# One transformer block on one Trainium2 core: the first tile's projections and front alone at the start, the other tiles' projections moved behind them

## What is computed

```python
n = rms_norm(h, g_mix)
proj = n @ w_in                                   # 2832 columns
gq, gk, gv, gz, gb, ga, sq, sk, sv = split(proj)  # gq, gk, gv: 3 x 512; the other 1296 are "token" columns
qkv = silu(causal_depthwise_conv(concat(gq, gk, gv), conv_w))      # 4 taps over tokens
o_gdn = gated_delta_net(qkv, gz, gb, ga)          # chunks of 64 tokens, a state carried over them
o_swa = sliding_window_attention(sq, sk, sv, rel_bias, sinks)
h = h + concat(o_gdn, o_swa) @ w_out
xn = rms_norm(h, g_ffn)
q = xn @ w_query                                  # 8 heads x 2 halves x 128
s1, s2 = q[0] @ keys1, q[1] @ keys2               # top 16 of 128 each, then top 16 of the 256 sums
eid, gate = ids_of(top16), softmax(top16)         # 8 x 16 = 128 experts a token
act = gelu(sum(expert_u[eid] * xn)) * gate        # one row of 1024 floats an expert and token
h = h + sum(act * expert_v[eid])
h = h + sigmoid(rms_norm(h, g_ple) @ w_gate) * (p @ w_proj)
```

## Time and profile before

| | |
|---|---|
| median of 3 runs (lowest, highest) | 3875.88 us (3864.65, 3882.54) |
| the profiled execution | 3871.93 us |
| its span, first to last instruction | 3870.1 us |
| busy: PE, DVE, ACT, POOL | 69%, 58%, 18%, 60% of the span |
| first gather issued | 540.9 us |

### The profile page before, as it was taken

One profiled execution on the slowest core, in us unless ns is written; L12 is line 12 of the kernel. 1 busy time (PEld: TensorE's weight loads), 2 busy tenths in 40 slices (PEclk: granted clock), 3 DMA queues, 4 the chain that ended last, 5 costly groups with the idle time before them and its releaser, 6 DMA issues.

```text
span 3870.1 us, 34568 instructions
## 1 busy us (share of the span) xinstructions
PE 2653.3 (69%) x11304; PEld 1342.1 (35%) x11304; DVE 2260.4 (58%) x5248; ACT 689.0 (18%) x1425; POOL 2309.9 (60%) x2052
## 2 busy tenths in 40 slices
PE   8997754766577657774767467855776577637777
PEld 4543542433243314331334134422432243313332
DVE  1123357558655865577656775586558665854554
ACT  2112321210112011201121112102210212002221
POOL 0000035747776767676766777677767776757774
PEclk9988777888788878887888787878888788868889
DMA  4322057979999999899999999999999999999996
GB/s 133 115 73 83 17 194 265 328 298 364 372 343 336 393 350 356 325 398 343 374 337 367 369 349 346 349 369 369 330 355 374 360 350 337 395 350 373 371 374 261
DMA packets 413901, 1213.70 MB, mean 314 GB/s; under 512 B 43680, under 2 KB 137888, under 8 KB 413600
## 3 DMA queue, kind: packets, MB, share of 16 engines
q0 software_dynamic: 294912, 1073.87, 73.6%
q1 hardware_dynamic: 118816, 137.69, 10.4%
HBM read 1190.64 MB, written 20.77 MB: 313 GB/s over the span
## 4 chain that ended last, share of the span: by engine, by line
PE 30%; POOL 19%; DMA 18%; issue 18%; DVE 12%; ACT 2%; SPq 1%; POOLq 0%; DVEq 0%; ACTq 0%
PE bank L920 20%; POOL v_rows L591 10%; DMA u_rows<-in_peer_u_dram,expert_id 9%; POOL u_rows L582 9%; PE expert_sum L920 8%; DMA w_query<-in_peer_w_query_dram 6%; DMA v_rows<-in_peer_v_dram,expert_id 3%; DVE u_rows L1780 3%; PE bank L923 2%; DVE arena L1713 1%; DVE arena L1719 1%; DVE arena L1722 1%; ACT L616 1%; ACT arena L616 1%; DVE arena L1677 0%
## 5 line engine op out<-in xcount | busy, mean ns | idle before, releaser
L582 POOL DMA_INDIRECT u_rows<-in_peer_u_dram,expert_id x1024 | 1159.9, 1133 | 858.3 <-ACT expert_id L821 540.4
L1780 DVE CUSTOM_DVE_ANT_0 u_rows<-u_rows,ffn_in 128x1024 f32<-128x1024 f32 x1024 | 1235.0, 1221 | 720.3 <-DMA u_rows<-in_peer_u_dram,expert_id 715.1
L920 PE MATMUL expert_sum<-v_rows,weight_diagonals 128*64 128x512 f32 x4096 | 1165.8, 708 | 601.0 <-DVE weight_diagonals L1765 452.9
L591 POOL DMA_INDIRECT v_rows<-in_peer_v_dram,expert_id x1024 | 1149.8, 1123 | 664.7 <-PE expert_sum L920 377.9
L920 PEld LDWEIGHTS expert_sum<-v_rows,weight_diagonals 128*64 128x64 f32 x4096 | 321.5, 158 | 1223.7 <-issue 1205.4
L920 PE MATMUL bank<-w_query,arena 128*128 128x256 f32 (+1 forms) x1088 | 316.9, 455 | 114.4 <-DMA w_query<-in_peer_w_query_dram 113.7
L923 PE MATMUL bank<-constants,arena 128*128 128x128 f32 x968 | 179.7, 332 | 298.9 <-DVE arena L1625 63.6
L920 PEld LDWEIGHTS bank<-w_query,arena 128*128 128x128 f32 x1088 | 238.3, 224 | 213.1 <-DMA w_query<-in_peer_w_query_dram 141.4
L920 PE MATMUL bank<-arena 128*128 128x128 f32 (+4 forms) x2176 | 269.9, 301 | 45.0 <-DVE arena L1530 28.8
L920 PEld LDWEIGHTS bank<-arena 128*128 128x128 f32 (+3 forms) x2176 | 251.5, 205 | 111.9 <-issue 65.5
L923 PEld LDWEIGHTS bank<-constants,arena 128*128 128x128 f32 x968 | 134.4, 169 | 418.1 <-issue 111.3
(11 more groups left out here) (167 smaller groups left out, 1977.4 us busy)
## 6 DMA issues: line engine op xcount, KB each, us to landing
w_query<-in_peer_w_query_dram SPq DMA_DIRECT2D x64, 1024.0 KB, 16.9
u_rows<-in_peer_u_dram,expert_id POOLq DMA_INDIRECT x1024, 6.9
v_rows<-in_peer_v_dram,expert_id POOLq DMA_INDIRECT x1024, 6.8
w_channel<-in_w_in_dram SPq DMA_DIRECT2D x12, 512.0 KB, 3.8
conv_scratch<-conv_out SPq DMA_DIRECT2D x12, 512.0 KB, 2.6
arena<-conv_scratch SPq DMA_DIRECT2D x8, 768.0 KB, 11.3
tok_scratch<-token_out SPq DMA_DIRECT2D x8, 648.0 KB, 3.3
arena<-tok_scratch SPq DMA_DIRECT2D x8, 648.0 KB, 13.9
```

The source lines that it names most:

```text
L582: nc.gpsimd.indirect_dma_start(u_ring[:, j, :], None, table_u, bass.IndirectOffsetOnAxis(id_of(q, j), 0)).then_inc(u_landed[j], 16)
L591: nc.gpsimd.indirect_dma_start(v_ring[:, j, :], None, table_v, bass.IndirectOffsetOnAxis(id_of(q, j), 0)).then_inc(v_landed[j], 16)
L920: return nc.tensor.matmul(out_, lhsT, rhs, start=start, stop=stop, **kw)
L1780: v.tensor_tensor_reduce(u_ring[:, j, :], u_ring[:, j, :], xb[:, j % NB, :], 1.0, 0.0, ALU.mult, ALU.add, hid[:, q % 2, j:j + 1]).then_inc ...
```

## The change

- SP first loads what tile 0 needs. Of the projections only tile 0's are done at the start: its 12 channel tiles over 128 tokens (96 products of 128 columns, into `conv0_in`, whose last three tokens are kept in `halo`), and its middle 512 token columns. The weights of these channels come in four loads into the places of `w_out_sb` and `w_query`.
- Parameters by channel come as rows and are turned by PE, not by strided loads; the keys are turned and the relative bias rows made at the start. The products with `g_mix` and with the inverse root move from DVE to POOL (two 128x1024 instructions a tile), the bias mask too.
- Tile 0's front starts then. The token projections (the rest of tile 0's, all of tiles 1 to 7) are cut into 45 steps (`token_steps`), and `fill` puts one ahead of the front's waits on PE and ACT; what is left runs ahead of piece 11. Their normed, turned rows are stored in `normed_scratch`. `expert_sum` is their PSUM buffer, so `finish_slots()` ends them before the rows for the dot products.
- The first gathers need two query pairs of tile 0, not four; pairs 2 and 3 follow the first gathers.
- The channel tiles of tiles 1 to 7 (12 tiles by 896 tokens) are put in periods 0 to 5, two a period, each half followed by `fill(2)`. Their source, `a_nT`, is loaded into `w_out_sb`; their weights (512 KB each) go through the `w_query` buffers, and the taps and silu work there too. `w_out` is loaded again behind them, and `front_loads(1)` only comes after the last channel store.
- The front of tile 1 starts in period 6, not 2, with two pieces in each of periods 6 to 10, and in 13.
- Tile 0's top-16 searches: one `best_pair` in each of periods 0, 1 and 2.
- DVE's wait for a tile's gates stands ahead of the expert weights, no longer ahead of the dot products. Otherwise nothing of the order is changed from period 16 on.

```diff
@@ front_piece
-                return {2: (0, 1), 8: (7, 8), **{i: (i - 1,) for i in range(3, 8)},
-                        **{i: (i,) for i in range(9, NG - 1)}}.get(g, ())
+                return {6: (0, 1), 7: (2, 3), 8: (4, 5), 9: (6, 7), 10: (8, 9), 11: (10,), 12: (11,), 13: (12, 13), 14: (14,)}.get(g, ())
@@ sync
+            sp.wait_ge(h1_mm, 2)
+            for u in range(2):
+                sp.wait_ge(rows_stored[u], 16 * ((LT + u) // 2))
+            sp.dma_start(a_nT, nT_dram.rearrange("t p (c n) -> p t c n", n=P)).then_inc(wch_loaded[2], 16)
...
+            sp.wait_ge(query_mm, NQ - 1)
+            for ct in range(2):
+                load_w_channel(ct)
+            for ct in range(NCT):
+                sp.wait_ge(a_channels_mm, channels_done(ct, 1))
+                if ct + 2 < NCT:
+                    load_w_channel(ct + 2)
+                if ct:
+                    store_channels(ct - 1)
+            load_w_out()
+            store_channels(NCT - 1)
+            for u in range(2):
+                sp.wait_ge(a_conv_stored[u], 16 * NCT // 2)
@@ gpsimd
+                nc.gpsimd.tensor_tensor(a_n[u][:], a_x[u][:], g_mix_b[:], ALU.mult).then_inc(a_n_ready, 1)
+                pool.wait_ge(a_n_ready, 2 * t + 1)
+                pool.wait_ge(x_inverse, t + 1)
+                nc.gpsimd.tensor_scalar(a_n[u][:], a_n[u][:], a_rs[:, t:t + 1], None, ALU.mult).then_inc(a_n_ready, 1)
...
+            pool.wait_ge(a_tok_stored, 16 * LT)
@@ tensor
+            def token_steps():
+
+                pe.wait_ge(keysT_ready, 4)
+                pe.wait_ge(a_w_loaded[0], 16)
+                project(acc_half[0], 0, 0, (0,))
+                yield
+                project(acc_half[0], 0, 0, (1,)).then_inc(a_tok_mm, 1)
+                yield
+                pe.wait_ge(a_w_loaded[2], 16)
+                project(acc_half[1], 0, 2).then_inc(a_tok_mm, 1)
+                yield
+                for t in range(1, NT):
+
+                    pe.wait_ge(a_tok_ready, tokens_before(t))
+                    turn_tile(t, acc_half)
+                    yield
+                    pe.wait_ge(a_nT_ready, 2 * t + 2)
+                    for n in range(2):
+                        project(acc_half[n], t, n, (0,))
+                        yield
+                        project(acc_half[n], t, n, (1,)).then_inc(a_tok_mm, 1)
+                        yield
+                    pe.wait_ge(a_tok_ready, tokens_before(t) + 1)
+                    project(acc_half[0], t, 2).then_inc(a_tok_mm, 1)
+                    yield
+
+            def channels(ct):
+                u = ct % 2
+                pe.wait_ge(wch_loaded[u], 16 * (u + 1) + 16 * (ct // 2 + 1))
+                if ct == 0:
+                    pe.wait_ge(wch_loaded[2], 32 + 16)
+                    pe.wait_ge(scores_ready, NQ)
...
+                for half, (t0, n) in enumerate(((0, 4), (4, LT - 4))):
                     for c in range(DC):
...
+                        last = mm(bank[2 * u + half][:, 0:n * P].rearrange("p (t n) -> p t n", n=P), a_wc[u][:, c, :],
+                                  a_nT[:, t0:t0 + n, c, :], c == 0, c == DC - 1)
                     last.then_inc(a_channels_mm, 1)
...
+                    fill(2)
...
-            for piece in pieces:
+            for piece in pieces[:11]:
                 piece(0)
+            finish_slots()
             rows_to_pairs(0)
             ids_to_pairs(1, first)
+
+            pe.wait_ge(ids_ready, 1)
+            for pair in range(2, 4):
+                query_pair(0, pair)
             pe.wait_ge(first_gates, 1)
             gates_to_pairs(first)
+            price = 2
             for q in range((NT - 1) * NG):
                 t = q // NG + 1
                 slots = expert_slots(q - 1) if q else iter(())
                 credit = 0
+                for ct in channel_tiles(q):
+                    channels(ct)
@@ vector
                 begin(q)
+                if 0 < q <= CHANNEL_PERIODS:
+                    conv(CP * q - 1)
+                if q < 3:
+                    best_pair(0, q + 1)
...
+                for ct in channel_tiles(q)[:-1]:
+                    conv(ct)
```

More of the change, by code:

```diff
@@ L670, in _ @@
-            for h in range(NH):
-                act.wait_ge(rel_mm, h + 1)
-                nc.scalar.copy(rel_rows[:, h, :], bank[4 + h % 2][:, 0:RELS]).then_inc(rel_rows_ready, 1)
-            with act.Fori(1, QKV // P // 2) as pair:
-                channel_pair(pair * 2)
-            act.wait_ge(params_b, 16 * 9)
-            f(neg_rate[:], a_rate[:], ACT.Exp).then_inc(rate_exp, 1)
+                copy_out(keysT[:].rearrange("p (h f) n -> p f h n", f=2)[:, half, h0:h0 + 4, :],
+                         acc[:, b % 2 * 512:b % 2 * 512 + 512].rearrange("p (h n) -> p h n", n=P)).then_inc(keysT_ready, 1)
@@ L679, in norm_root, with fill, finish_tokens @@
+            tokens = token_steps()
+            def fill(n):
+                for _ in range(n):
+                    next(tokens, None)
+            def finish_tokens():
+                for _ in tokens:
+                    pass
             def norm_root(n, ap):
@@ L728, in level @@
             def level(t, l):
+                fill(1)
                 for r in range(2):
@@ L771, in piece10 @@
             def piece10(t):
+                fill(6)
                 for b in range(4):
@@ L1264, in expert_slots @@
                     yield
-            slots = iter(())
-            credit = 0
+            slots = token_steps()
+            credit, price = 0, 1
             def fill(n):
```

646 lines of the change are left out of this document (394 added, 252 removed).

## The result

The changed kernel takes 3786.2 us (median of 4 runs, 3777.4 to 3791.6), the kernel before in the same job 3876.8 (4 runs, 3864.7 to 3882.5). The ratio is 0.9768, 95% interval 0.9738 to 0.9798: faster by 90.6 us, where the forecast was 104 and the range 3700 to 3835.

The account below looks back on a forecast made before the run. DMA was taken to bound settled tiles, PE the part ahead of the gathers. Gain 226 less losses 48 + 30 + 29 + 15 = 122 gave net 104: 3768, or 3772 against the median, range 3700 to 3835.

Parts of the forecast that it names:

- Start of the front: Tile 0's front starts at 55 us, between 50 and 65, with POOL's two elementwise instructions a tile hidden.
- The front with steps in it: Tile 0's front with token steps takes 205 us, bounds 190 and 242: PE work 49 plus 138, and 18 of waits.
- First gather: First gather at 315 us (55 + 205 + 55), 226 earlier than 540.9.
- the two other pairs drop out of the path: Ahead of the first gather: query pairs 2 and 3 (20.5 us) leave the path, 55 us after 471.5 against 69.4.
- Pace of the channel tiles: Periods 0 to 5: PE takes 31.6 us a period, plus 10 for DVE's long period 2.
- The slower rival: SP's one queue paces the channel tiles, deciding from 27 us a tile; kernel 116 slower, 3992; chance 0.06.
- My bound of 12 to 23 us: Periods 0 to 5: a pair of 512 KB weight blocks lands under gathers in 12 to 23 us, inside 31.6.
- the loss of periods 0 to 5: Period 5 ends on PE 220 us after the first gather, against 172 before: loss 48, bounds 35 and 75.
- Period 6: Stall before tile 1's piece 0, store queued behind `w_out`: 40 us on PE, loss 30, bounds 10 and 55.
- Periods 6 to 15: Tile 1's chain sets the length, 187 us from piece 0 against 158: loss 29; period 13's searches and pick: loss 15.
- The fast rival: Queue stays ahead, loop near DMA's pace, first gather at 295: net 210, 3666 us; chance 0.06.
- The front's steps do not hide: Rival for tile 0's front: front 242, first gather 352, net 30 to 50, 3825 to 3850 us; chance 0.09.

Follow-up runs that it names:

- the bare front: Changed kernel with all 45 token steps run as one block ahead of tile 0's front, nothing woven in: 3833.8 us, ratio 0.9895.
- the run with all four pairs: Changed kernel with all four query pairs of tile 0 done before the first gather: ratio 0.9665.
- the kernel with four pairs and the late `w_out`: Changed kernel with four query pairs before the first gather and `w_out` loaded behind the last store and tile 1's first loads: 3743.7 us, 0.9657.
- the moved searches: Changed kernel with tile 1's pieces 10 and 11 in period 11, pieces 12 and 13 in periods 12 and 13: 3776.3 us, 0.9744.
- the late `w_out`: Changed kernel with the second load of `w_out` issued behind the last channel store and tile 1's first loads: ratio 0.9732.
- the early rows: Changed kernel with the load of the turned rows issued ahead of the last six `w_query` blocks: ratio 0.9708.

## Why the prediction was right, point by point

- **Start of the front.** Predicted 55, measured 55.45. That POOL's two instructions stay hidden was right. Their price, which had no row, is 2.34 us for the product of two operands and 2.85 for the one with a scalar, 5.2 a tile, inside the bounds of 2.1 to 8.5; against DVE's 1.38 (4.14 for three) and 0.75 that is 1.7 and 3.8 times.

```profile
10.08 2.34 POOL L634 TENSOR_TENSOR x_normed<-x_in,g_mix_rows 128x1024 f32<-128x1024 f32 x1 [9.64 <-DMA rel_bias_sb<-in_rel_bias_dram]
12.51 2.85 POOL L637 TENSOR_SCALAR x_normed<-x_normed,small 128x1024 f32<-128x1024 f32 x1
```

  The page that the prediction cites (GPSIMD Engine Reference of the Trainium skill, 4.1) has two inputs about twice as slow; the trace agrees roughly, with 1.7. For one input the page has roughly the line rate; the trace does not agree, with 3.8 times DVE's duration, and the measurement decides.
- **The front with steps in it.** Predicted 205, measured 264.8 - 55.4 = 209.4. The choice between PE sums at either clock was right: the windows stand at 0.90, 1.00 and 0.98, and the front's own products took 48.4 us of PE (predicted 49; bare 62.1). The waits left over were 15.9 us, predicted 18; the token work was 145.1, predicted 138. The clock was low where PE stood waiting for much of a stretch: 0.69 from 317 to 371, 0.59 from 561 to 589, and 0.75 in the bare front. That is what the cited rule says (Trainium skill, TensorE: Matmul & The Clock Gate, HAM oscillation: a PE that keeps stopping falls back), and the trace agrees: the front was not such a PE any more.
- **First gather.** 317.4 against 315. The step "the two other pairs drop out of the path" brings the gather 13.7 us forward, as the run with all four pairs shows, and the forecast counted 69.4 - 55 = 14.4 us of gain for it (the 20.5 us that it names are PE's work, and less of that lay on the path). For the whole it is a loss: the loads behind it cost more (next but one point).
- **Pace of the channel tiles.** Predicted 24 + 5 x 31.6 + 10 = 192 us from the first to the last, measured 190.0; periods 4 and 5 are 32.0 and 32.3. Leaving out half of the products shows PE to be the cause. The slower rival (the queue paces them) needed 27 us a channel tile; a tile took some 16, and loads and stores land in 7.3 and 6.7 us:

```profile
w_query<-in_w_in_dram SPq DMA_DIRECT2D x12, 512.0 KB, 7.3
...
conv_scratch<-w_query SPq DMA_DIRECT2D x12, 448.0 KB, 6.7
```

  My bound of 12 to 23 us came from loads in stretches with DMA shares of 1.02 and 1.04 (834 to 866 and 882 to 906 of the kernel before); these run in one of 0.91. With half the products, where the share is 1.01 to 1.04, such a load takes 16.4 us, inside the bound.
- **The mis-sized start.** "PE's first channel tile starts about 28 us after the first gather": it was 53.6. This is the step of the periods 0 to 5 that failed: 25.6 us, which puts the end of the channel tiles at +243.6 against the predicted +220. I had taken the last query pairs and the weights as PE time and left out that their loads, and the 3.5 MB of turned rows, are issued together with 16 gathers; PE's three waits for them sum to 27.9 us. Loading the rows earlier gives 11 us of it back, and issuing all of it before the first gather gives back all. By the forecast's own points on PE the loss of periods 0 to 5 is 243.6 - 172 = 71.6, against 48. I also left out that the gathers stand still behind the first channel tiles, as the wait of 56 us on POOL shows; no run puts the experts of period 0 ahead of those tiles with the first gather where it is, so what that alone costs stays open.
- **Period 6.** The predicted mechanism is there: `w_out` ahead of the store ahead of the load, PE's gap 26.7 us with a predicted 40. From the last channel product at 561.0 to piece 0 it is 28.5 us, 1.8 of them an expert product: 12.3 us of taps and silu (the store is issued at 573.3), 11.3 until the load from `conv_scratch` is issued, and 5.0 until it has landed. Only the middle part is the queue's: the store lands in 11.2 us behind `w_out`, and in 2.4 when issued ahead of it (in the kernel with four pairs and the late `w_out`). That agrees with the rule that the prediction cited from the Trainium skill (DMA: Bandwidth & Descriptors), consumption in ring order; but as `w_out` had 10.5 us of start by then, only its rest was waited for. I had priced all of it. Its 20.6 us from issue to landing lie inside my 12 to 45; the 182 GB/s that I named beside them follow from no row (the load came to 204).
- **Periods 6 to 15.** Predicted 30 + 29 + 15 = 74 with the stall, measured 71.7 on POOL's marks: 34.7 in periods 6 to 10 and 37.0 in 11 to 15. My terms have their bounds elsewhere, since the second query pair (piece 10) now falls in period 11. PE's rows show them. The keys' product that ends the second query pair, before and after:

```profile
870.61 0.71 PE L920 MATMUL bank<-keys_by_channel,arena 128*128 128x128 f32 x4
```

```profile
785.51 0.71 PE L1085 MATMUL bank<-keys_by_channel,arena 128*128 128x128 f32 x4
```

  From piece 0 (589.55) to there it is 196.7 us, predicted 187. With the stall it is 225.2 from the last channel product, against 158.4 before from the forecast's mark (540.9 + 172), a loss of 66.8 against 30 + 29. From there to period 16 it is 119.5 us against 126.5, 7.0 less, where I had 15 more. Two searches in a period do cost what I took, as the moved searches show (17 to 18 us); but piece 10 now lies in period 11, not 10, so one period less stands behind it, and I had not counted that. PE waits for a `w_query` block in period 11 of POOL's marks (49.8 us long) and for DVE's searches and pick in period 14 (43.5):

```profile
768.64 6.66 PE L1085 MATMUL bank<-w_query,arena 128*128 128x256 f32 x16 [5.61 <-DMA w_query<-in_peer_w_query_dram]
...
863.60 8.65 PE L1085 MATMUL expert_sum<-v_rows,weight_diagonals 128*64 128x512 f32 x32 [27.68 <-DVE weight_diagonals L1988]
```

  That block's load holds the chain that ended last for longer than PE's wait shows:

```profile
755.47 13.13 DMA w_query<-in_peer_w_query_dram
```

  Whether the length of tile 1's chain, experts' work included, or the pieces put two in a period sets these ten periods was not separated by any run: I neither shortened the chain nor gave each search a period of its own in this kernel. How much of the 71.7 us can be had back stays open.
- **The fast rival** (loop near DMA pace, first gather 295) fell on both counts. **The front's steps do not hide** fell at the front, where 209 stands against its 242. The kernel without hiding takes 3834 us, inside that rival's 3825 to 3850, but not by its terms: the first gather is at 370, not 352, and the periods behind it lose no more than in the changed kernel.
- **A reading of the slices.** DMA reaches nine tenths in the eighth slice, not the sixth or seventh, and stands at 7 tenths in the seventh and the ninth. No term rests on it.

So the gain is: 223.5 at the first gather, less 59.7, less 71.7, less 7.7 in parts that the change does not touch. That the total came within 20 us of the forecast, by the spans, is in part luck. In the forecast's own terms the start and pace of the channel tiles lost 23.6 us more than it said, stall and chain 7.8 more, the first gather came 2.5 later and the rest took 7.7 more; the 22.0 us between the 15 lost and the 7.0 gained behind the second query pair cancel half of that.

## What to carry to other kernels

When serial, half-idle work stands ahead of a loop that is bound by bandwidth, independent products put into its waits pay twice: they disappear, and they keep PE's clock up. Here that was 53 us at the first gather for 145 us of products, with PE's clock at 0.98 over the front and not 0.75; a part of the 53 is idle time of the block that they made when run ahead.

Here it paid to hold the bandwidth-bound stream back until the loads that the next critical chain needs had landed. An earlier first gather (13.7 us) made the chain's next products 38 us late, and gathers let loose during a stall made a 5 us load take 20. The versions that let the loads go first were faster: 0.9657 against 0.9767 in the same job (with the late `w_out`, which on top of the early rows brought nothing by period 16), and 0.9657 against 0.9710 on different chips.

Look at who waits while an engine is busy all the time. PE, busy without a break from 371 on, hid 40 us in which DMA moved 42 GB/s, because the products that free the gathers' buffers stood behind two channel tiles in PE's list.

A delay that moves along when two pieces are moved together does not tell crowding from a long chain. For that, one run must give each piece a period of its own and change nothing else.

## What the runs showed of the hardware that I had not expected

- SP's queue gets a small part of the rate beside the indirect gathers: 71 of 382 GB/s in the 20 us in which 768 KB and 648 KB were loaded beside them, 238 without them. The 3.5 MB of turned rows landed in 11.7 us ahead of the gathers (314 GB/s), and in 39.7 beside them and behind two 1 MB blocks.
- POOL's instruction with one operand of 128x1024 and a scalar (2.85 us) takes longer than the one with two operands (2.34).
